# Taking 1 - beta of stick-breaking attention from the scores by a sigmoid of their negative

## The chip, the cores and the metric

The program is one decoder layer and runs on one core of a Trainium2 chip. The time is device microseconds (us) from the start of the program to its end. Below, TensorE is PE in the rows (its weight loads are PEld), ScalarE is ACT, VectorE is DVE, GpSimd is POOL and SyncE is SP.

## The reference, cut to what matters

A layer has three mixers (chunked gMLP, gated DeltaNet, stick-breaking attention), a gated merge and a feed-forward part. The change is in attention alone: 8 heads of 64, 1024 positions, swept in blocks of 128 queries.

```python
# A[t,s] = beta[t,s] prod_{s<j<t} (1-beta[t,j]), beta = sigmoid(q.k/sqrt(dh)), s<t
z = jnp.einsum('bthd,bshd->bhts', qi, kf) * scale          # scale = 64 ** -0.5
causal = kpos[None, :] < tpos[:, None]
log_keep = jnp.where(causal, jax.nn.log_sigmoid(-z), 0.0)
later = lax.cumsum(log_keep, axis=3, reverse=True) - log_keep
w = jnp.where(causal, jnp.exp(jax.nn.log_sigmoid(z) + later), 0.0)
return jnp.einsum('bhts,bshd->bthd', w, vf)
```

The kernel works with the products themselves. For each score it needs beta = sigmoid(z) and the factor that it calls keep, 1 - beta, which equals sigmoid(-z). A scan from the right multiplies the keeps, and beta times the product of the later keeps is the weight.

## The kernel before, in words

Weights come from HBM in 512 KB pieces, are split by ACT into an upper part (`w_hi`, L308) and by DVE into a rest (`w_lo`, L313), and each product of the large matrices is three matmuls (L321 to L323). These products run through the whole kernel. The other mixers' work is laid between them.

Attention is a loop of four passes, each over two heads (u = 0 and 1). A pass has 12 pieces of scores: the query blocks in `ORDER`, each with up to 512 keys, so 128 to 512 columns. All engines walk the same steps x = -2 to 12 of a pass, written out by hand, each in its own queue, and wait for each other through counting semaphores:

- PE (L1070 on): in step x the scores of piece x + 2 into `z0` and `z1` (`scores`, one PSUM bank for each head), in the first step also the transposes of v (`turn_values`) into `dn0` and `dn1`, the weighted values of piece x - 1 (`weighted_values`), a share of the matrix products (`pe_beside`), the transposes of piece x (`turn`), and another share of products. The banks `z0` and `z1` are single: from the second piece of a pass on `scores` waits at L1077 until the previous piece has been read. That is 11 waits in a pass, 44 in all.
- ACT (L769 on): `sigmoid` (L777) reads `z` and writes `a_b`, for both heads of piece x + 2. In the first step of a pass two copies of the turned values follow (L805, PSUM to `a_v`). Then `keep` (L784) reads `a_b` and writes `a_keep`, and for each head `take_turned` (L791) follows it and waits for the transposes of piece x. Then come the evictions of the products (L363) and the `w_hi` splits that fall due (`act_beside`).
- DVE (L1414 on): for piece x + 1 the two scans over `a_keep` (L1426), the two products with `a_b` (`weigh`, L1436), the mask, then the `w_lo` splits (`dve_beside`). At the end of a pass and between pieces it copies finished output (`take_y`, L1452).
- SP only loads weights and stores and loads projections. ACT sends the attention output away (L795).

`a_b`, `a_keep` and `a_A` have four buffers each, two pieces. At the start of each pass ACT has an `ACT_TABLE_LOAD` ahead of its first sigmoid.

Of the kernel before, what the change touches and what calls it, by code (L numbers as in the profile page):

```python
# [58 lines left out]
def hybrid_decoder_layer(nc, xT, w_stream, w_bd, w_spT, cols_in, consts_in, outT):  # L59
    f32, f32r, bf16 = mybir.dt.float32, mybir.dt.float32r, mybir.dt.bfloat16  # L60
    ACT, ALU = mybir.ActivationFunctionType, mybir.AluOpType
# [9 lines left out]
    def sb(name, shape, dt=f32):  # L71
        return scope[0].enter_context(nc.sbuf_tensor(name, shape, dt))

    def sem(name):
        return top.enter_context(nc.semaphore(name))

    with top:
# [71 lines left out]
        with scope[0]:  # L149
# [4 lines left out]
            a_b = [sb(f"a_b{s}", [P, HALF]) for s in range(4)]  # L154
            a_keep = [sb(f"a_keep{s}", [P, HALF]) for s in range(4)]
# [56 lines left out]
        def bank(name):  # L212
            return top.enter_context(nc.psum_tensor(name, [P, HALF], f32))

        g_bank = [bank("gemm0"), bank("gemm1")]
        z_bank = [bank("z0"), bank("z1")]
# [37 lines left out]
        z_ready, b_ready, keep_ready, p_ready, a_raw, a_ready = (  # L254
            sem(n) for n in ("z_ready", "b_ready", "keep_ready", "p_ready", "a_raw", "a_ready"))
# [218 lines left out]
        NST = 2 * NBK  # L474
        LEAD = 2
# [222 lines left out]
        def _(act):  # L698
# [70 lines left out]
            with act.Fori(0, 4) as i:  # L769
                b = Beside(PAIR_AT + 2 * i, AT_SLOTS, (ACT.Identity,) * 2)  # L770

                def sigmoid(y):
                    n = block_of(y // 2)[3]
                    act.wait_ge(z_ready, NST * i + y + 1)
                    if y >= 4:
                        act.wait_ge(a_ready, NST * i + y - 3)
                    nc.scalar.activation(a_b[y % 4][:, 0:n], z_bank[y % 2][:, 0:n], ACT.Sigmoid, scale=0.125).then_inc(b_ready, 1)  # L777

                def keep(y):
                    n = block_of(y // 2)[3]  # L780
                    act.wait_ge(b_ready, NST * i + y + 1)
                    if y >= 4:
                        act.wait_ge(p_ready, NST * i + y - 3)
                    nc.scalar.activation(a_keep[y % 4][:, 0:n], a_b[y % 4][:, 0:n], ACT.Identity, scale=-1.0, bias=1.0).then_inc(keep_ready, 1)  # L784

                def take_turned(y):
                    x, u = divmod(y, 2)
                    n = block_of(x)[3]
                    act.wait_ge(turned, NST * i + y + 1)
                    act.wait_ge(av_done, 1 + NBK * i + x - 1)  # L790
                    nc.scalar.activation(a_AT[u][x % 2][:, 0:n], d_bank[u][:, 0:n], ACT.Copy).then_inc(at_read, 1)  # L791

                def store_y(T):
                    act.wait_ge(av_read, 2 + 8 * i + (4 if T else 8))
                    act.dma_start(yT[8 + i, :, HALF * T:HALF * T + HALF], a_y[:, HALF * T:HALF * T + HALF]).then_inc(y_stored[T], 16)  # L795

                for x in range(-LEAD, NBK + 1):
                    if x + LEAD < NBK:
                        for u in range(2):
                            sigmoid(2 * (x + LEAD) + u)  # L800
                    if x == -LEAD:
                        for hf in range(2):
                            act.wait_ge(at_vt, 2 * i + hf + 1)
                            act.wait_ge(av_done, 1 + NBK * i)
                            nc.scalar.activation(a_v[:, 4 * hf:4 * hf + 4, :], d_bank[hf][:].rearrange("p (n c) -> p n c", c=P),  # L805
                                                 ACT.Copy).then_inc(at_v, 1)
                    for u in range(2):
                        if x + LEAD < NBK:
                            keep(2 * (x + LEAD) + u)
                        if 0 <= x < NBK:  # L810
                            take_turned(2 * x + u)
                    act_beside(act, b)
                    act_beside(act, b)
                    if x == LAST_OF[3] + 3:
                        store_y(1)
                store_y(0)
# [69 lines left out]
            for b in range(4):  # L886
                for hf in range(2):
                    x = 2 * b + hf
# [24 lines left out]
            for i in range(2):  # L913
                for q in range(6):
                    n, s = PAIR_BR + 3 * i + q // 2, q % 2
# [97 lines left out]
        def _(pe):  # L1013
# [56 lines left out]
            with pe.Fori(0, 4) as i:  # L1070
                b = Beside(PAIR_AT + 2 * i, AT_SLOTS, (ACT.Identity,) * 2)

                def scores(x):

                    blk, p, s0, n, off = block_of(x)
                    if x:
                        pe.wait_ge(b_ready, NST * i + 2 * x)  # L1077
                    for u in range(2):
                        h = slice(64 * u, 64 * u + 64)
                        nc.tensor.matmul(z_bank[u][:, 0:n], a_q[h, P * blk:P * blk + P], a_k[h, s0:s0 + n],  # L1080
                                         start=True, stop=True).then_inc(z_ready, 1)

                def turn_values():

                    pe.wait_ge(vT_loaded, 16 * i + 16)
                    pe.wait_ge(at_read, 1 + NST * i)
                    for hf in range(2):
                        for n in range(4):
                            last = nc.tensor.transpose(d_bank[hf][:, P * n:P * n + P], a_vT[:, P * (4 * hf + n):P * (4 * hf + n) + P], ident)
                        last.then_inc(at_vt, 1)  # L1090

                def turn(y):

                    x, u = divmod(y, 2)
                    n = block_of(x)[3]
                    pe.wait_ge(a_ready, NST * i + y + 1)
                    if x == 0:
                        pe.wait_ge(at_v, 2 * i + u + 1)
                    else:
                        pe.wait_ge(at_read, 1 + NST * i + y - 1)  # L1100
                    for m in range(n // P):
                        last = nc.tensor.transpose(d_bank[u][:, P * m:P * m + P], a_A[y % 4][:, P * m:P * m + P], ident)  # L1102
                    last.then_inc(turned, 1)

                def weighted_values(x):

                    blk, p, s0, n, off = block_of(x)
                    pe.wait_ge(at_read, 1 + NST * i + 2 * x + 2)
                    if newest(x):
                        pe.wait_ge(av_read, 2 + 8 * i + p - 1)  # L1110
                    for m in range(n // P):
                        for u in range(2):
                            last = nc.tensor.matmul(y_bank[p % 2][64 * u:64 * u + 64, 0:P], a_v[:, s0 // P + m, 64 * u:64 * u + 64],
                                                    a_AT[u][x % 2][:, P * m:P * m + P], start=(newest(x) and m == 0),
                                                    stop=(oldest(x) and m == n // P - 1), skip_group_check=True)
                    last.then_inc(av_done, 1)

                pe.wait_ge(at_loaded, 32 * i + 32)
                for x in range(-LEAD, NBK + 1):
                    if x + LEAD < NBK:  # L1120
                        scores(x + LEAD)
                    if x == -LEAD:
                        turn_values()
                    if x >= 1:
                        weighted_values(x - 1)
                    pe_beside(pe, b)
                    if 0 <= x < NBK:
                        turn(2 * x)
                        turn(2 * x + 1)
                    pe_beside(pe, b)  # L1130
            leave_phase(pe)

            with pe.Fori(0, 4) as i:
# [18 lines left out]
                for x, name in enumerate(DN_STAGES):  # L1152
                    for g in range(2):
# [10 lines left out]
                        for m in range(4):  # L1164
                            n = 4 * g + m
# [63 lines left out]
            for b in range(4):  # L1229
                pe.wait_ge(g_chain, 13 + 4 * b + 2)  # L1230
                for hf in range(2):
                    if b:
                        pe.wait_ge(g_act, 8 + 2 * b)
                    for m in range(4):
                        n = 4 * hf + m
# [15 lines left out]
            for i in range(2):  # L1251
                for q in range(6):
                    n, s = PAIR_BR + 3 * i + q // 2, q % 2
                    pe.wait_ge(lo_ready[s], n + 1)
                    for r in range(4):
# [3 lines left out]
                        for k in range(4):  # L1259
                            kk, y = 4 * dd + k, 4 * (q % 3) + k  # L1260
# [56 lines left out]
        def _(dve):  # L1317
# [96 lines left out]
            with dve.Fori(0, 4) as i:  # L1414
# [14 lines left out]
                def weigh(y):  # L1429

                    x, u = divmod(y, 2)
                    blk, p, s0, n, off = block_of(x)
                    dve.wait_ge(p_ready, NST * i + y + 1)
                    if y >= 4:
                        dve.wait_ge(turned, NST * i + y - 3)
                    nc.vector.tensor_tensor(a_A[y % 4][:, 0:n], a_b[y % 4][:, 0:n], a_P[u][p % 2][:, off + 1:off + n + 1],  # L1436
                                            ALU.mult).then_inc(a_raw if newest(x) else a_ready, 1)
# [145 lines left out]
            for b in range(4):  # L1583
# [5 lines left out]
                y = g_y[b % 2]  # L1589
                if b >= 2:  # L1590
                    dve.wait_ge(g_store[b % 2], 16)
                for hf in range(2):
                    t = slice(HALF * hf, HALF * hf + HALF)
                    dve.wait_ge(g_pe, 10 + 4 * b + 2 + hf + 1)
                    bias = cols[:, None, V_BSP + P * b:V_BSP + P * b + P].broadcast_to([P, 4, P])
# [8 lines left out]
            for i in range(2):  # L1604
                for q in range(6):
                    n, s = PAIR_BR + 3 * i + q // 2, q % 2
# [264 lines left out]
```

## Time and profile before

| | |
|---|---|
| Time, median of 3 runs (lowest, highest) | 2145.39 us (2144.16, 2149.23) |
| The profiled execution's own time | 2151.76 us |
| Its span | 2149.9 us |
| PE busy, share of the span | 2014.6 us, 94% |
| ACT busy | 765.0 us, 36% |
| DVE busy | 934.9 us, 43% |
| Mean granted TensorE clock | 0.975 |
| Attention, first to last scores | 167.1 to 464.8 us after the span's start |

Busy shares are averages over the whole layer. PE is close to full nearly everywhere, so an instruction elsewhere matters only if PE ends up waiting for it. The views of waits say for whom an engine waited, the timeline gives the order with starts and durations, and the views by stretch give the granted clock, where 1.00 is 2.4 GHz and 0.50 is 1.2 GHz.

### The profile page before, as it was taken

Reading aid. Unit: us, or ns where it says so; the run is one execution under the profiler, and the core shown is the slowest. Engines: PE = TensorE matmul, PEld = TensorE weight load, DVE = VectorE, ACT = ScalarE, POOL = GpSimd, SP = SyncE. Lnnn points to the kernel's source line nnn. Section 1 sums busy time; section 2 is a strip of 40 time slices with the busy share of each in tenths; the row PEclk is TensorE's granted clock in tenths of the full one; section 3 lists DMA queues with packets and bytes.
Section 4 is the critical chain, followed back from the end, with each engine's and each line's share of the span. In section 5 each row is a group of like instructions: output and inputs, shape, how many; then the busy total and the mean of one; then the engine's idle time right before and its main releaser. Section 6 shows DMA issues by size and latency. Waiting matters only on the chain.

```text
span 2149.9 us, 27155 instructions
## 1 busy us (share of the span) xinstructions
PE 2014.6 (94%) x9986; PEld 1610.2 (75%) x9986; DVE 934.9 (43%) x1291; ACT 765.0 (36%) x1176; POOL 77.1 (4%) x63
## 2 busy tenths in 40 slices
PE   7999999999999999998798997988999999999996
PEld 5886776677878778787486886766888888888875
DVE  5715456455344272442144553565323323322346
ACT  5325555444343343532134333444113202202331
POOL 0000000000202002030000000000000000000000
PEclk9999999999999999999899998989999999999998
DMA  4232222213021030211425444322211111111143
GB/s 167 98 108 70 86 76 73 88 59 137 21 94 72 29 117 21 96 39 49 176 99 196 138 137 147 118 95 92 69 49 47 52 49 39 52 46 49 49 166 118
DMA packets 59624, 186.95 MB, mean 87 GB/s; under 512 B 6448, under 2 KB 6448, under 8 KB 59568
## 3 DMA queue, kind: packets, MB, share of 16 engines
q1 hardware_dynamic: 56112, 179.91, 23.7%
q10 hardware_dynamic: 3456, 6.29, 0.8%
q8 instruction: 36, 0.59, 0.1%
q14 instruction: 20, 0.16, 0.0%
HBM read 140.04 MB, written 46.14 MB: 87 GB/s over the span
## 4 chain that ended last, share of the span: by engine, by line
PE 76%; DVE 8%; ACT 6%; DMA 5%; issue 5%; SPq 1%; DVEq 0%; ACTq 0%
PE gemm L321 16%; PE gemm L323 15%; PE gemm L322 15%; DMA w_raw<-w_stream 3%; PE gemm L536 3%; PE gemm L537 3%; PE gemm L538 3%; PE dn L1184 2%; ACT w_hi L308 2%; PE z L1080 2%; PE dn L1182 2%; PE gemm L1263 2%; PE gemm L1264 2%; PE gemm L1265 2%; PE dn L1102 1%
## 5 line engine op out<-in xcount | busy, mean ns | idle before, releaser
L321 PE MATMUL gemm<-act_hi,w_hi 128*128 128x512 f32 x1216 | 513.6, 422 | 7.8 <-ACT stage L363 7.1
L323 PE MATMUL gemm<-act_hi,w_lo 128*128 128x512 f32 x1216 | 478.8, 394 | 0.0
L322 PE MATMUL gemm<-act_lo,w_hi 128*128 128x512 f32 x1216 | 477.8, 393 | 0.0
L313 DVE TENSOR_TENSOR w_lo<-w_raw,w_hi 128x1024 fp32r<-128x1024 f32 x166 | 204.5, 1232 | 403.8 <-ACT w_hi L308 399.9
L308 ACT ACTIVATE w_hi<-w_raw 128x1024 fp32r<-128x1024 f32 x166 | 174.8, 1053 | 342.3 <-PE gemm L323 229.9
L321 PEld LDWEIGHTS gemm<-act_hi,w_hi 128*128 128x128 f32 x1216 | 231.4, 190 | 67.9 <-issue 21.3
L323 PEld LDWEIGHTS gemm<-act_hi,w_lo 128*128 128x128 f32 x1216 | 230.1, 189 | 50.2
L322 PEld LDWEIGHTS gemm<-act_lo,w_hi 128*128 128x128 f32 x1216 | 231.5, 190 | 44.3 <-issue 6.5
L363 ACT ACTIVATE stage<-gemm,cols 128x512 f32<-128x512 f32 x104 | 71.2, 685 | 230.8 <-PE gemm L323 224.9
L321 PE MATMUL gemm<-f_hi,w_hi 128*128 128x512 f32 x384 | 149.5, 389 | 0.0
L323 PE MATMUL gemm<-f_hi,w_lo 128*128 128x512 f32 x384 | 149.5, 389 | 0.0
L322 PE MATMUL gemm<-f_lo,w_hi 128*128 128x512 f32 x384 | 149.5, 389 | 0.0
L536 PE MATMUL gemm<-act_hi,w_hi 128*128 128x512 f32 x256 | 107.6, 420 | 32.6 <-DVE w_lo L313 21.7
L965 ACT ACTIVATE f_t<-f_t 128x512 f32<-128x512 f32 x64 | 40.3, 630 | 203.3 <-DVE f_t L1686 203.3
L1426 DVE TENSOR_TENSOR_SCAN a_P<-a_keep,a_P,a_floor 128x512 f32<-128x512 f32 (+3 forms) x96 | 93.9, 1006 | 29.5 <-ACT a_keep L784 29.4
L537 PE MATMUL gemm<-act_lo,w_hi 128*128 128x512 f32 x256 | 103.5, 404 | 0.0
L538 PE MATMUL gemm<-act_hi,w_lo 128*128 128x512 f32 x256 | 103.1, 403 | 0.0
L1789 POOL TENSOR_TENSOR d_bB<-d_at,consts 128x512 f32<-128x512 f32 x48 | 64.3, 1354 | 888.8 <-DVE d_at L1535 801.6
L1686 DVE SCALAR_TENSOR_TENSOR f_t<-gemm,sum_x 128x512 f32<-128x512 f32 x64 | 44.2, 691 | 110.1 <-PE gemm L323 91.3
L1692 DVE TENSOR_TENSOR f_lo<-f_t,f_hi 128x512 f32 (+1 forms) x64 | 44.3, 693 | 102.2 <-ACT f_hi L967 102.2
L536 PEld LDWEIGHTS gemm<-act_hi,w_hi 128*128 128x128 f32 x256 | 50.4, 197 | 50.3 <-DVE w_lo L313 25.1
L1263 PE MATMUL gemm<-y_hi,w_hi 128*128 128x512 f32 x192 | 77.4, 403 | 9.0 <-DVE y_lo L404 7.7
(247 smaller groups left out, 2950.5 us busy)
## 6 DMA issues: line engine op xcount, KB each, us to landing
w_raw<-w_stream SPq DMA_DIRECT2D x166, 512.0 KB, 3.5
projections<-stage SPq DMA_DIRECT2D x60, 512.0 KB, 2.9
gate<-projections SPq DMA_DIRECT2D x48, 256.0 KB, 2.7
d_in<-projections SPq DMA_DIRECT2D x12, 512.0 KB, 5.0
y_lo<-branch_outputs SPq DMA_DIRECT2D x6, 1024.0 KB, 12.0
x_sb<-xT SPq DMA_DIRECT2D x8, 512.0 KB, 9.6
x_fin<-xT SPq DMA_DIRECT2D x8, 512.0 KB, 8.5
residual<-mixed ACTq DMA_DIRECT2D x16, 256.0 KB, 2.0
```

What stands on the lines that cost most here:

```text
L308: nc.scalar.activation(hi[s][:], raw[s][:].rearrange("p (k c) -> p k c", k=KT), ACT.Copy).then_inc(hi_ready[s], 1)
L313: nc.vector.tensor_tensor(lo[s][:], raw[s][:].rearrange("p (k c) -> p k c", k=KT), hi[s][:].bitcast(f32), ALU.subtract).then_inc(lo_ready[ ...
L321: nc.tensor.matmul(g_bank[hf][:], w_hi[s][:, k, :], a_hi[:, k, t], start=(k == 0), stop=False)
L322: nc.tensor.matmul(g_bank[hf][:], w_hi[s][:, k, :], a_lo[:, k, t], start=False, stop=False)
L323: last = nc.tensor.matmul(g_bank[hf][:], w_lo[s][:, k, :], a_hi[:, k, t], start=False, stop=(k == KT - 1))
L363: nc.scalar.activation(stage[s][:, HALF * hf:HALF * hf + HALF], g_bank[hf][:], func, bias=cols[:, ds(V_BIN + 2 * n + s, 1)]).then_inc(bank ...
L536: nc.tensor.matmul(g_bank[s][:], w_hi[s][:, k, :], a_hi[:, k, t], start=(k == 0), stop=False)
L537: nc.tensor.matmul(g_bank[s][:], w_hi[s][:, k, :], a_lo[:, k, t], start=False, stop=False)
L538: last = nc.tensor.matmul(g_bank[s][:], w_lo[s][:, k, :], a_hi[:, k, t], start=False, stop=(k == KT - 1))
L1263: nc.tensor.matmul(g_bank[hf][:], w_hi[s][:, kk, :], y_upper(y)[:, t], start=(k == 0), stop=False)
L1426: nc.vector.tensor_tensor_scan(run[:, off:off + n][:, ::-1], a_keep[y % 4][:, 0:n][:, ::-1], floor[:, ::-1], run[:, off + n:off + n + 1], ...
L1789: nc.gpsimd.tensor_tensor(d_B[:, c, :], d_at[:, c, :], consts[:, None, C_LEV + lev, :].broadcast_to([P, 4, P]), ALU.mult).then_inc(dn_b[g], 1)
```

## The change

`keep` is now a sigmoid of the scores times -0.125, read from PSUM like beta, and no longer an affine function of `a_b`. It waits for `z_ready` and not for `b_ready`. On ACT the calls of `sigmoid` and `keep` change places, so that both keeps of a piece come first and the betas follow. PE must wait for both before it overwrites `z`, and DVE's `weigh` waits for `b_ready` itself.

```diff
@@ ACT, in the loop of the four passes @@
                 def keep(y):
                     n = block_of(y // 2)[3]
-                    act.wait_ge(b_ready, NST * i + y + 1)
+                    act.wait_ge(z_ready, NST * i + y + 1)
                     if y >= 4:
                         act.wait_ge(p_ready, NST * i + y - 3)
-                    nc.scalar.activation(a_keep[y % 4][:, 0:n], a_b[y % 4][:, 0:n], ACT.Identity, scale=-1.0, bias=1.0).then_inc(keep_ready, 1)
+                    nc.scalar.activation(a_keep[y % 4][:, 0:n], z_bank[y % 2][:, 0:n], ACT.Sigmoid, scale=-0.125).then_inc(keep_ready, 1)
...
                 for x in range(-LEAD, NBK + 1):
                     if x + LEAD < NBK:
                         for u in range(2):
-                            sigmoid(2 * (x + LEAD) + u)
+                            keep(2 * (x + LEAD) + u)
                     if x == -LEAD:
...
                     for u in range(2):
                         if x + LEAD < NBK:
-                            keep(2 * (x + LEAD) + u)
+                            sigmoid(2 * (x + LEAD) + u)
                         if 0 <= x < NBK:
                             take_turned(2 * x + u)
@@ PE, scores @@
                     if x:
                         pe.wait_ge(b_ready, NST * i + 2 * x)
+                        pe.wait_ge(keep_ready, NST * i + 2 * x)
@@ DVE, weigh @@
                     dve.wait_ge(p_ready, NST * i + y + 1)
+                    dve.wait_ge(b_ready, NST * i + y + 1)
```

ACT at the start of the first pass, before. `a_b` is beta, `a_v` the turned values, `dn` the banks with the transposes:

```order
L777 ACT_TABLE_LOAD
L777 ACTIVATE a_b0<-z0 128x128 [waits z_ready]
L774 REGISTER_ALU
L777 ACTIVATE a_b1<-z1 128x128 [waits z_ready]
L803 ISA
L804 ISA [waits at_vt]
L805 ACTIVATE a_v<-dn0 128x512 [waits av_done]
L803 REGISTER_ALU
L805 ACTIVATE a_v<-dn1 128x512 [waits av_done,at_vt]
L784 ACTIVATE a_keep0<-a_b0 128x128 [waits b_ready]
L784 ACTIVATE a_keep1<-a_b1 128x128 [waits b_ready]
```

The same place of ACT in the changed kernel:

```order
L784 ACT_TABLE_LOAD
L784 ACTIVATE a_keep0<-z0 128x128 [waits z_ready]
L781 REGISTER_ALU
L784 ACTIVATE a_keep1<-z1 128x128 [waits z_ready]
L803 ISA
L804 ISA [waits at_vt]
L805 ACTIVATE a_v<-dn0 128x512 [waits av_done]
L803 REGISTER_ALU
L805 ACTIVATE a_v<-dn1 128x512 [waits av_done,at_vt]
L777 ACTIVATE a_b0<-z0 128x128 [waits z_ready]
L777 ACTIVATE a_b1<-z1 128x128 [waits z_ready]
```

The last reader of `z0` and `z1` stood ahead of the two copies to `a_v` and now stands behind them.

ACT in the third step of a pass (x = 0), before. `a_AT` is the transposed weights of piece 0:

```order
L774 REGISTER_ALU
L777 ACTIVATE a_b0<-z0 128x256 [waits a_ready,z_ready]
L774 REGISTER_ALU
L777 ACTIVATE a_b1<-z1 128x256 [waits a_ready,z_ready]
L784 ACTIVATE a_keep0<-a_b0 128x256 [waits p_ready,b_ready]
L791 ACTIVATE a_AT00<-dn0 128x128 [waits av_done,turned]
L784 ACTIVATE a_keep1<-a_b1 128x256 [waits p_ready,b_ready]
L791 ACTIVATE a_AT10<-dn1 128x128 [waits av_done,turned]
```

The same step of ACT in the changed kernel:

```order
L781 REGISTER_ALU
L784 ACTIVATE a_keep0<-z0 128x256 [waits p_ready,z_ready]
L781 REGISTER_ALU
L784 ACTIVATE a_keep1<-z1 128x256 [waits p_ready,z_ready]
L777 ACTIVATE a_b0<-z0 128x256 [waits a_ready,z_ready]
L791 ACTIVATE a_AT00<-dn0 128x128 [waits av_done,turned]
L777 ACTIVATE a_b1<-z1 128x256 [waits a_ready,z_ready]
L791 ACTIVATE a_AT10<-dn1 128x128 [waits av_done,turned]
```

The second beta, a reader of `z1`, now stands where the second keep stood, behind the copy that waits for PE's transposes.

PE at the second scores of a pass, before:

```order
L323 MATMUL gemm0<-act_hi,w_lo0 128x512
L1077 REGISTER_ALU
L1080 MATMUL z0<-a_k,a_q 128x512 [waits b_ready]
L1080 MATMUL z1<-a_k,a_q 128x512
L321 MATMUL gemm0<-act_hi,w_hi0 128x512
```

And PE there in the changed kernel, one line further down in the file:

```order
L323 MATMUL gemm0<-act_hi,w_lo0 128x512
L1077 REGISTER_ALU
L1081 MATMUL z0<-a_k,a_q 128x512 [waits keep_ready,b_ready]
L1081 MATMUL z1<-a_k,a_q 128x512
L321 MATMUL gemm0<-act_hi,w_hi0 128x512
```

PE's order stays; the first matmul of the scores waits for two semaphores.

## Rows read from the trace of the kernel before

**Rows 1.** The page, busy us, share of the span, instructions.
```profile
PE 2014.6 (94%) x9986; PEld 1610.2 (75%) x9986; DVE 934.9 (43%) x1291; ACT 765.0 (36%) x1176; POOL 77.1 (4%) x63
```

**Rows 2.** By stretch, first and last pass: length, engines' busy us, PEclk, DMA, GB/s.
```profile
165.00:242.00 77.00, 76.25 (x467) 54.63 (x466) 44.59 (x82) 41.35 (x87) 0.00 (x0) 1.00 0.22 80
...
396.00:473.00 77.00, 75.25 (x456) 54.05 (x454) 43.39 (x75) 40.90 (x85) 0.00 (x0) 0.98 0.16 58
```

**Rows 3.** Waits of PE, 160 to 480 us: total us, times, longest.
```profile
PE z L1080 <- ACT a_b L777: 5.7, 4, 1.8
```

**Rows 4.** Waits of ACT, 160 to 480 us.
```profile
ACT a_AT L791 <- PE dn L1102: 84.0, 48, 2.5
...
ACT L777 <- DVE a_y L1452: 7.2, 3, 2.4
```

**Rows 5.** Waits of DVE, 160 to 480 us.
```profile
DVE w_lo L313 <- ACT w_hi L308: 103.4, 17, 9.3
DVE a_P L1426 <- ACT a_keep L784: 29.4, 24, 3.9
```

**Rows 6.** Timeline of ACT, start of pass 1: start us, us, what.
```profile
171.30 0.45 ACT L777 ACTIVATE a_b<-z 128x128 f32<-128x128 f32 x2
...
172.59 0.53 ACT L784 ACTIVATE a_keep<-a_b 128x128 f32<-128x128 f32 x2
```

**Rows 7.** Timeline of ACT, start of pass 2; in brackets idle before, releaser.
```profile
247.57 1.28 ACT L777 ACT_TABLE_LOAD   x1 [2.41 <-DVE a_y L1452]
248.86 0.45 ACT L777 ACTIVATE a_b<-z 128x128 f32<-128x128 f32 x2
249.19 1.09 ACT L805 ACTIVATE a_v<-dn 128x512 f32<-128x512 f32 x2
250.15 0.53 ACT L784 ACTIVATE a_keep<-a_b 128x128 f32<-128x128 f32 x2
```

**Rows 8.** Timeline of PE, second scores of each of the four passes.
```profile
171.80 1.13 PE L1080 MATMUL z<-a_k,a_q 64*128 64x512 f32 x4 [0.41 <-ACT a_b L777]
...
249.36 1.13 PE L1080 MATMUL z<-a_k,a_q 64*128 64x512 f32 x4 [1.77 <-ACT a_b L777]
...
326.90 1.13 PE L1080 MATMUL z<-a_k,a_q 64*128 64x512 f32 x4 [1.75 <-ACT a_b L777]
...
404.48 0.70 PE L1080 MATMUL z<-a_k,a_q 64*128 64x512 f32 x2 [1.75 <-ACT a_b L777]
```

**Rows 9.** The tiles `a_b` and `a_keep`, durations ns: least, median, most.
```profile
L777 ACT ACTIVATE a_b<-z x96: 272/551/628, 171.3 to 465.3; 128x512 f32<-128x512 f32 x48, 128x128 f32<-128x128 f32 x16, 128x256 f32<-128x256 f32 x16, 128x384 f32<-128x384 f32 x16
L784 ACT ACTIVATE a_keep<-a_b x96: 302/588/669, 172.6 to 468.5; 128x512 f32<-128x512 f32 x48, 128x128 f32<-128x128 f32 x16, 128x256 f32<-128x256 f32 x16, 128x384 f32<-128x384 f32 x16
```

**Rows 10.** Timeline of ACT, third step of pass 2.
```profile
257.83 0.28 ACT L791 ACTIVATE a_AT<-dn 128x128 f32<-128x128 f32 x1 [0.73 <-PE dn L1102]
258.01 0.41 ACT L784 ACTIVATE a_keep<-a_b 128x256 f32<-128x256 f32 x1
```

**Rows 11.** Timeline of PE's weight loads, fourth scores of pass 2.
```profile
258.54 0.30 PEld L1080 LDWEIGHTS z<-a_k,a_q 64*128 64x128 f32 x4 [0.36 <-issue]
```

**Rows 12.** By stretch, columns as in rows 2: five stretches behind an idle PE.
```profile
249.37:255.41 6.04, 6.04 (x26) 4.16 (x27) 4.86 (x10) 4.01 (x9) 0.00 (x0) 1.00 0.00 1
326.91:332.99 6.08, 6.08 (x26) 4.16 (x27) 4.90 (x10) 4.00 (x9) 0.00 (x0) 1.00 0.00 1
404.49:412.14 7.65, 7.65 (x26) 5.33 (x26) 5.30 (x10) 4.00 (x9) 0.00 (x0) 0.78 0.00 1
...
499.39:506.20 6.81, 6.81 (x19) 5.39 (x20) 6.36 (x6) 3.57 (x4) 0.00 (x0) 0.59 0.19 77
...
1180.09:1186.90 6.81, 6.74 (x22) 5.12 (x23) 4.17 (x5) 1.21 (x2) 0.00 (x0) 0.75 0.14 43
```

**Rows 13.** Timeline of PE, the matmuls that open two of those stretches.
```profile
499.38 0.79 PE L321 MATMUL gemm<-act_hi,w_hi 128*128 128x512 f32 x1 [4.62 <-ACT stage L363]
...
1180.08 0.51 PE L1263 MATMUL gemm<-y_hi,w_hi 128*128 128x512 f32 x1 [1.50 <-DVE y_lo L404]
```

## The prediction

> **What bounds the kernel now.** I read the page first: TensorE is busy 94% of the span and ScalarE 36% [rows 1], so a ScalarE instruction counts only where TensorE waits for it. The view by stretch, laid over the passes of attention, says the same of the place of the change: of the first pass's 77.00 us TensorE is busy 76.25, ScalarE 41.35, VectorE 44.59, and the last pass differs only in its clock [rows 2]. The views of waits came next. In attention TensorE waits for other engines in one place alone, the scores: 5.7 us in 4 waits, all for beta [rows 3]. ScalarE spends 84.0 us waiting for TensorE's transposes [rows 4], VectorE 103.4 us for `w_hi` and 29.4 us for `a_keep` [rows 5]; none of that is passed on. The timeline then shows that the 4 waits are the second scores of each pass, with 0.41, 1.77, 1.75 and 1.75 us of idle TensorE ahead of them [rows 8]. There ScalarE goes through a table load, two betas, two copies to `a_v`, two keeps [rows 6, 7], and TensorE starts when the second beta is done: the pair ends at 248.86 + 0.45 = 249.31, the scores begin at 249.36, so 0.05 us pass from release to start.
>
> **The operation itself.** Per piece two affine functions from SBUF become two sigmoids from PSUM, 96 instructions in all. For equal shapes the nearest row is beta, which is the same instruction already: 272 against 302 ns for the shortest, 551 against 588 for the median [rows 9]. That is 0.03 to 0.04 us less each, 3 to 4 us of ScalarE's time, and nothing for the end, since ScalarE waits 84.0 us for transposes anyway. If that cover were gone, the 3 to 4 us would be a gain and no loss. The table load stays one in a pass: both versions call the sigmoid first.
>
> **The order on ScalarE at the start of a pass.** This is the term that costs. The last reader of `z0` and `z1` was the second beta, ahead of the copies; it becomes the second beta behind them. The second keep stands there now: in pass 1 the pair ends at 172.59 + 0.53 = 173.12, in pass 2 at 250.15 + 0.53 = 250.68 [rows 6, 7]. Taking off 0.03 for the shorter instruction and adding 0.05 for the release, the scores begin at 173.14 and 250.70 instead of 171.80 and 249.36 [rows 8]: 1.34 us later. From the other side, with the measured length of a beta pair instead: 250.15 + 0.45 + 0.05 = 250.65, 1.29 us later. TensorE is idle already at that point, so all of it adds, and in pass 1 too. Four passes give 5.2 to 5.4 us; I take 5.3. The copies themselves wait for nothing new. What stands behind the waiting scores in TensorE's queue is matrix products, and everybody else in the pass waits on TensorE, so nothing makes the time good later. ScalarE's release at the start of the next pass hangs on the last `a_y` copy [rows 4], which follows TensorE as well.
>
> **The order on ScalarE inside a pass.** The keeps come first where the betas stood, and the betas take the keeps' places. The second beta now stands behind the copy to `a_AT` that waits for TensorE's transposes. The other 40 scores wait for it. The narrowest place that I found is the fourth scores of a pass: the copy begins at 257.83, the second keep at 258.01 and ends at 258.42 [rows 10], and the weights of the scores load at 258.54 [rows 11]. That leaves 0.12 us, less 0.05 for the release, plus 0.03 for the shorter instruction: 0.10 us to spare. So 40 waits at nothing. Covered they are by the products between the transposes and the next scores; without that cover each would cost what its beta is late, and the upper bound that I keep is one release, 0.05 us, at each of 40, so 2.0 us.
>
> **The added waits.** TensorE's wait for `keep_ready` is satisfied before the one for `b_ready`, since both keeps are done ahead of the first beta; nothing. VectorE's `weigh` waits for beta, which comes two scans later than it needs; its scans can start about one beta pair earlier, up to 1.1 us, and VectorE's 29.4 us of waiting for `a_keep` shrinks. TensorE never waits for `a_A` in attention [rows 3], so I put this at nothing too, and below nothing only by the rival at the end.
>
> **The clock.** The granted clock is no constant. Behind the 1.75 us of idle in pass 4 it was 0.78 in the mean over 7.65 us, where the same 26 matmuls of pass 2, behind 1.77 us of idle, took 6.04 us at 1.00 [rows 8, 12]. So a fall to 1.2 GHz costs 7.65 - 6.04 = 1.6 us, and it came once in three such gaps. Behind 1.50 us elsewhere it was 0.75 over 6.81 us, which is (1 - 0.75) x 6.81 = 1.7 us, and behind 4.62 us it was 0.59, or 2.8 us [rows 12, 13]. The change lengthens the gaps of passes 2 to 4 to 3.1 us and that of pass 1 to 1.7 us. I expect a fall behind each of the three, 3 x 1.6 = 4.8, a third of one in pass 1, 0.5, and take off the 1.6 that this execution has already paid: +3.7 us. The ends are no fall at all, -1.6, and four falls at 2.8, 11.2 - 1.6 = +9.6.
>
> The Trainium skill speaks of this in "TensorE: Matmul & The Clock Gate", section "HAM oscillation": its rule of thumb names a length of idle gap beyond which the engine starts again at the low clock, and the gaps forecast here stay below it. By that rule there would be no clock term, and the sum would be about 5 us. The trace bears it out in two passes of three and not in pass 4, where a shorter gap was followed by a fall. It is among the rivals. Another page speaks against the change altogether: "Perfetto Trace Analysis", section "Optimizing Tensor Performance", wants independent matmul groups to rotate through PSUM banks so that the eviction of one overlaps the next. Holding `z` for a second read goes against that at each of the 44 scores, and by the rule I would have counted a beta pair, 1.1 us, at each, some 48 us; the rows say that ScalarE's second read is in time at 40 of them.
>
> **The sum.** 5.3 + 3.7 = 9.0 us on the profiled execution's 2151.76 us (span 2149.9 and 1.86 around it), so 2160.8. The median of the runs lies 6.4 us lower, and the change should add about the same there: 2145.39 + 9.0 = 2154.4. A measurement of this kernel can tell a change from none beyond about 0.3%, here 6.4 us.
>
> **The rivals.**
> - The clock does not answer to the longer gaps: only the 5.3 us of waiting are added, 2150.7. For it: two of three gaps of 1.75 us went without a fall [rows 12]. Against: behind 1.50 us it fell elsewhere, and 3.1 is twice that. Chance 0.22; this case is within 0.3%.
> - The added wait is hidden, because the release of the second scores does not come from the place in the queue that I read, or is given back where TensorE waits later: 0 us, 2145.4. Against: TensorE is already idle at this point in all four passes [rows 8]. Chance 0.07.
> - Betas late inside the pass too: the 0.10 us margin fails and TensorE waits at the 40 inner scores. At 0.05 each 2 us, and if ScalarE runs a tenth of a microsecond or more late, 4 to 6: 9.0 + 5 = 14, 2159.4. For it: the narrow margin. Against: the place of the second keep was in time each time. Chance 0.08.
> - Faster: VectorE, with its scans earlier, finishes a pass earlier, and the last `a_y` copy, for which ScalarE's start of the next pass waits 7.2 us in all [rows 4], comes forward so far that the second scores wait no more. Then the four gaps of 5.7 us and the one fall of 1.6 go: -7.3, 2138.1. It turns into a gain only once the copy comes more than 1.3 us earlier. Against: at the end of a pass VectorE waits for `w_hi` and the copy stands behind that, which the scans don't touch. Chance 0.03.
> - The forecast itself, +9.0 within 7 to 12: chance 0.60.
>
> Slower by over 0.3%: 0.60 + 0.08 and a little of the first rival's upper part, less a little of the forecast's lower part, 0.67. Within 0.3%: 0.30. Faster: 0.03. The range goes from 2148.0, which keeps most of the case without clock term, to 2160.5, which takes in falls of 2.8 us; the outer bounds worked out above are +3.6 and +17.0 (5.4 + 9.6 + 2.0).
>
> **What would show it.** At the second scores of each pass the gap ahead of TensorE is 1.7 us in pass 1 and 3.1 us in passes 2 to 4, and its releaser is beta; the total of that wait is near 11 us instead of 5.7. The granted clock of the stretch behind is near 0.78 in passes 2 to 4, and the stretch about 7.6 us long. Keeps have beta's durations. ScalarE's row order at a pass start is keeps, `a_v`, betas. VectorE's wait for `a_keep` shrinks, and its work ends no sooner in the passes. No other scores wait. I am wrong if the first gap stays, if any of the other 40 scores waits for `a_b`, or if TensorE waits anywhere else that it did not.

## The result, and the profile after

| | before | changed |
|---|---|---|
| Time, median (lowest, highest) | 2147.31 us (2144.16, 2150.97), 4 runs | 2167.14 us (2166.14, 2170.39), 4 runs |
| Ratio, 95% interval | | 1.0094 (1.0073 to 1.0116) |
| Profiled execution: time, span | 2151.76, 2149.9 us | 2167.50, 2165.7 us |
| Attention, first to last scores | 297.50 us | 311.65 us |
| The rest of the span | 1852.4 us | 1854.1 us |

The change made the kernel 19.8 us slower, where 9.0 were forecast; the range ended at 2160.5. The direction was right and the size was not. A second measurement, below, gave 1.0064 (1.0050 to 1.0077), or 14.3 us. Attention is counted from the start of the first scores in pass 1 to the start of the last scores in pass 4.

The first line is the page's, for [rows 1]:

```profile
PE 2020.4 (93%) x9986; PEld 1612.3 (74%) x9986; DVE 934.6 (43%) x1291; ACT 762.9 (35%) x1176; POOL 77.2 (4%) x63
```

ScalarE's busy time fell by 2.1 us, as cheaper keeps should make it. TensorE's rose by 5.8 us with the same number of instructions: the same matmuls took longer. In attention alone its busy time went from 291.81 to 300.66 us, 8.9 more. That is the first sign of the clock.

The waits of PE, ACT and DVE in the changed kernel between 160 and 495 us (total us, times, longest), for [rows 3 to 5]:

```profile
PE z L1081 <- ACT a_b L777: 11.0, 4, 3.1
```
```profile
ACT a_AT L791 <- PE dn L1103: 85.4, 48, 2.6
...
ACT L784 <- DVE a_y L1454: 7.2, 3, 2.4
```
```profile
DVE a_P L1427 <- ACT a_keep L784: 29.6, 12, 3.8
...
DVE a_A L1438 <- ACT a_b L777: 3.2, 8, 0.5
```

TensorE still waits for beta in 4 places, now for 11.0 us in place of 5.7: 5.3 more, the forecast's first term to the tenth. Timelines of PE at the second scores and of ACT ahead of those of pass 2, for [rows 7, 8]:

```profile
174.28 0.70 PE L1081 MATMUL z<-a_k,a_q 64*128 64x512 f32 x2 [1.75 <-ACT a_b L777]
...
254.77 1.22 PE L1081 MATMUL z<-a_k,a_q 64*128 64x512 f32 x2 [3.09 <-ACT a_b L777]
...
336.55 1.22 PE L1081 MATMUL z<-a_k,a_q 64*128 64x512 f32 x2 [3.07 <-ACT a_b L777]
...
418.38 1.22 PE L1081 MATMUL z<-a_k,a_q 64*128 64x512 f32 x2 [3.07 <-ACT a_b L777]
```
```profile
251.66 1.28 ACT L784 ACT_TABLE_LOAD   x1 [2.41 <-DVE a_y L1454]
252.95 0.45 ACT L784 ACTIVATE a_keep<-z 128x128 f32<-128x128 f32 x2
253.28 1.09 ACT L805 ACTIVATE a_v<-dn 128x512 f32<-128x512 f32 x2
254.24 0.48 ACT L777 ACTIVATE a_b<-z 128x128 f32<-128x128 f32 x2
```

Keeps, copies, betas: the betas end at 254.24 + 0.48 = 254.72 and the scores start at 254.77. What was not forecast is in the view by stretch. Each row goes from the second scores to the third, for [rows 12] (length, busy us by engine, then PEclk, DMA, GB/s):

```profile
174.28:181.94 7.66, 7.66 (x26) 5.31 (x26) 4.43 (x8) 2.75 (x5) 0.00 (x0) 0.78 0.03 11
254.77:263.74 8.97, 8.97 (x26) 5.84 (x26) 4.42 (x8) 2.76 (x5) 0.00 (x0) 0.65 0.00 0
336.55:345.57 9.02, 9.02 (x26) 5.85 (x26) 4.42 (x8) 2.75 (x5) 0.00 (x0) 0.64 0.00 0
418.38:427.44 9.06, 9.06 (x26) 5.88 (x26) 4.42 (x8) 2.75 (x5) 0.00 (x0) 0.64 0.00 0
```

The work of a stretch takes 6.04 us at full clock. Here the four take 34.71 us, 10.6 more than 4 x 6.04 = 24.16. Before, the four stretches took 25.82 us, 1.6 more, for one fall. So 34.71 - 25.82 = 8.9 us come from the clock, and 5.3 + 8.9 = 14.2 is the difference of attention, 311.65 - 297.50. The rest of the two spans differs by 1.7 us.

### The profile page after: what moved, and what is told of

Its sections match the earlier page's. It is cut to its first block, busy times and chain, and to the rows that moved or that the text cites. A ratio compares the mean times of both kernels' runs of the same rounds, so it can differ in the third digit from the quotient of the medians.

```text
span 2165.7 us, 27215 instructions
## 1 busy us (share of the span) xinstructions
PE 2020.4 (93%) x9986; PEld 1612.3 (74%) x9986; DVE 934.6 (43%) x1291; ACT 762.9 (35%) x1176; POOL 77.2 (4%) x63
## 4 chain that ended last, share of the span: by engine, by line
PE 75%; DVE 8%; ACT 6%; issue 5%; DMA 5%; SPq 1%; DVEq 0%; ACTq 0%
PE gemm L321 16%; PE gemm L323 15%; PE gemm L322 15%; DMA w_raw<-w_stream 3%; PE gemm L536 3%; PE gemm L538 3%; PE gemm L537 3%; PE dn L1185 2%; PE z L1081 2%; ACT w_hi L308 2%; PE dn L1183 2%; PE gemm L1264 2%; PE gemm L1265 2%; PE gemm L1266 2%; DVE d_cv L1491 1%
## 5 line engine op out<-in xcount | busy, mean ns | idle before, releaser
L1427 DVE TENSOR_TENSOR_SCAN a_P<-a_keep,a_P,a_floor 128x512 f32<-128x512 f32 (+3 forms) x96 | 92.2, 1002 | 29.6 <-ACT a_keep L784 29.6
```

Source lines behind the costliest of these rows:

```text
L1427: nc.vector.tensor_tensor_scan(run[:, off:off + n][:, ::-1], a_keep[y % 4][:, 0:n][:, ::-1], floor[:, ::-1], run[:, off + n:off + n + 1], ...
```

## The experiments

Theory A: the last reader of `z` stands behind the two copies at the start of a pass, TensorE idles longer there, and the granted clock falls behind the longer gap. Rivals: B, a price inside the pass (the second read of PSUM, the second wait, betas behind the transposes' copies); C, the exchange of places as such; D, another cause of the long stretches; E, one fixed cost. Times "within 3 us of the changed kernel" are told by ratios to the kernel before in the same measurement. The changed kernel has two of them, 1.0094 and 1.0064. The second ran on one chip with the moved products, the first four experiments on another, and of the first the chip is not on record.

### Betas ahead of the copies

```diff
                     if x == -LEAD:
+                        for u in range(2):
+                            sigmoid(u)
                         for hf in range(2):
                             act.wait_ge(at_vt, 2 * i + hf + 1)
...
-                        if x + LEAD < NBK:
+                        if x > -LEAD and x + LEAD < NBK:
                             sigmoid(2 * (x + LEAD) + u)
```

> The changed kernel, with one difference: in the first step of a pass the two betas come ahead of the two copies to a_v (keeps, betas, copies). Everything inside the pass is as in the changed kernel. Theory A (the loss is the place of the last reader of z at the start of a pass, and the clock that answers to the longer gap): the second scores are released by the second beta, two short instructions or 0.35 us later than in the kernel before, so TensorE's wait for beta at the four second scores is 5.7 + 4 x 0.35 = 7.1 us instead of 11.0, the stretch behind each is 6.0 to 7.7 us instead of 9.0, and the time is +2 to +7 us on the kernel before, 12 to 17 below the changed kernel. Theory B (the loss comes from inside the pass: two reads of PSUM, the second wait of the scores, betas behind the transposes' copies): nothing of that is altered, so the time stays within 3 us of the changed kernel.

Measured: 2148.72 us against 2147.12, ratio 1.0005 (0.9994 to 1.0016). Waits of PE, and the stretch from second to third scores in passes 2 and 3:

```profile
PE z L1083 <- ACT a_b L777: 7.1, 4, 2.1
```
```profile
246.11:252.15 6.04, 6.04 (x26) 4.16 (x26) 4.76 (x9) 3.68 (x7) 0.00 (x0) 1.00 0.00 0
323.98:330.02 6.04, 6.04 (x25) 4.17 (x25) 4.77 (x9) 3.69 (x7) 0.00 (x0) 1.00 0.00 0
```

The wait is the 7.1 us that theory A gave, and the clock did not fall behind any of the four gaps. The time came out a little better than its +2. That there was no fall was luck, since the kernel before has one in each of its traces behind shorter gaps. Attention took 297.19 us: the 297.50 of before, 1.4 of added waiting, and 1.6 less for the fall that did not come, within 0.1. Everything inside the pass was as in the changed kernel, so this takes B's place away: all that the change does there costs nothing that can be measured.

### Keep from the scores, in its old place

```diff
 def keep(y):
-    act.wait_ge(b_ready, NST * i + y + 1)
+    act.wait_ge(z_ready, NST * i + y + 1)
-    nc.scalar.activation(a_keep[y % 4][:, 0:n], a_b[y % 4][:, 0:n], ACT.Identity, scale=-1.0, bias=1.0)
+    nc.scalar.activation(a_keep[y % 4][:, 0:n], z_bank[y % 2][:, 0:n], ACT.Sigmoid, scale=-0.125)
 # PE, scores: waits for b_ready and keep_ready; DVE, weigh: waits for b_ready; order on ACT as before
```

> The kernel before with keep as a sigmoid of the negated scores from PSUM, but in its old place behind beta (and behind the copies to a_v at the start of a pass). TensorE waits for both, as in the changed kernel. Theory A: the last reader of z stands behind the copies here too, so it costs the same as the change: wait at the second scores 11 us, stretches behind of 9.0 us in passes 2 to 4, time within 3 us of the changed kernel. If the exchange of places on ScalarE by itself were what costs (theory C), this kernel would stay within 3 us of the kernel before.

Measured: 2160.23 us, ratio 1.0059 (1.0040 to 1.0079). Waits of PE, and the four stretches:

```profile
PE z L1081 <- ACT a_keep L784: 11.0, 4, 3.1
```
```profile
170.51:176.55 6.04, 6.04 (x25) 4.16 (x25) 4.73 (x10) 2.76 (x5) 0.00 (x0) 1.00 0.06 24
249.39:257.05 7.66, 7.66 (x25) 5.33 (x25) 5.10 (x10) 2.75 (x5) 0.00 (x0) 0.78 0.00 0
329.87:338.81 8.94, 8.94 (x26) 5.80 (x26) 5.10 (x10) 2.75 (x5) 0.00 (x0) 0.65 0.00 0
411.62:420.64 9.02, 9.02 (x26) 5.85 (x26) 5.10 (x10) 2.75 (x5) 0.00 (x0) 0.65 0.00 0
```

Same wait, same kind of stretches, without the exchange of places. The stretch of pass 2 is 7.66 us where 9.0 was written down, and pass 1 has no fall. The time is within 3 us of the changed kernel by its second measurement, 1.0064, and not by its first, 1.0094. C is out even so, since it wanted the time of the kernel before: it does not matter which of the two stands last, only that the last one stands behind the copies.

### The wait alone

```diff
 # kernel before, PE, scores
     pe.wait_ge(b_ready, NST * i + 2 * x)
+    pe.wait_ge(keep_ready, NST * i + 2 * x)
```

> The kernel before, with one wait added: the scores on TensorE also wait for the previous piece's keep, which here is still the affine function of beta in SBUF, so no value depends on the wait. No second read of PSUM, no exchange of places. Theory A: the wait is released by the second keep behind the copies, 1.37 us after beta, so TensorE waits 11.1 us at the second scores and the time is within 3 us of the changed kernel (+18 to +22 us). Theory B (reading PSUM twice, or the sigmoid in place of the affine function): this kernel keeps the time of the kernel before, within 3 us.

Measured: 2162.78 us (2158.18 to 2166.74), ratio 1.0062 (1.0042 to 1.0082): 15.7 us slower, less than the 18 to 22 written down, which leaned on the first measurement of the change. Waits of PE, and the stretches of passes 1 and 2:

```profile
PE z L1081 <- ACT a_keep L784: 11.5, 4, 3.2
```
```profile
174.00:181.62 7.62, 7.62 (x25) 5.30 (x25) 4.98 (x10) 2.81 (x5) 0.00 (x0) 0.78 0.04 13
254.64:263.36 8.72, 8.72 (x26) 5.61 (x26) 4.98 (x10) 2.81 (x5) 0.00 (x0) 0.67 0.00 0
```

One wait, with no second read of PSUM and no new sigmoid, costs as much as the whole change: its attention takes 311.65 us, as the changed kernel's did. That the two agree to the hundredth is chance, for this kernel waits 0.5 us longer and its four stretches sum to 33.98 us instead of 34.71. B is out in its other half too.

### The changed kernel with the gap filled

```diff
 # PE, end of a step
     pe_beside(pe, b)
+    if x == -LEAD:
+        pe.wait_ge(av_read, 2 + 8 * i - 1)
+        for _ in range(10):
+            nc.tensor.matmul(o_bank[:], act_hi[:, 0, 0:P], act_hi[:, 0, 0:HALF], start=True, stop=True)
```

> The changed kernel, with 10 matmuls 128x128 by 512 added on TensorE between the first step's products and the second scores of each pass; their result goes to the idle output bank and is overwritten. They add 10 x 0.227 = 2.3 us of work and take no value. If the larger part of the loss is the clock that falls behind the gap (theory A), the gap falls from 3.1 to 0.8 us in passes 2 to 4 and vanishes in pass 1, where the scores start 0.5 us later; the stretch behind, from the second to the third scores, goes from 9.0 us to 6.0 in passes 2 to 4 and from 7.7 to 6.0 in pass 1; the time is 8 to 11 us below the changed kernel although TensorE does more. If the long stretches have another cause (ScalarE or a bank late behind the second scores, theory D), they stay at 9.0 and the time is the same as the changed kernel or up to 2 us longer.

Measured: 2152.80 us, ratio 1.0024 (1.0013 to 1.0035), against the changed kernel's 1.0064 in its second measurement: 0.4% or 8.6 us less, with 40 matmuls more. On its own chip it is 7.4 and 10.0 us below the two kernels that have the same wait, 1.0059 and 1.0062. Waits of PE, and two stretches:

```profile
PE z L1081 <- ACT a_b L777: 2.4, 3, 0.8
```
```profile
173.40:179.46 6.06, 6.06 (x26) 4.16 (x26) 3.98 (x6) 2.76 (x5) 0.00 (x0) 1.00 0.01 3
252.29:258.33 6.04, 6.04 (x25) 4.17 (x25) 4.42 (x8) 2.76 (x5) 0.00 (x0) 1.00 0.00 0
```

ScalarE's queue is the changed kernel's, the scores start as late as there, and the long stretches are gone: the clock was behind them, not a late bank (D). Attention takes 301.58 us, the sum of 295.9 (before without its fall), the 5.3 of the wait and the 0.4 us by which the filling overshoots in pass 1. That is 4.1 us over the attention of before, which has a fall to pay. The medians differ by 5.7 us, with an interval from 2.8 to 7.5 that takes in the 4.1.

### The changed kernel and the kernel before again

> The changed kernel once more, unaltered, for its spread on the chip that also runs the next kernels, and for a second trace. Waiting is fixed by the program and the clock is not: the gaps at the second scores are 1.75, 3.1, 3.1, 3.1 us again, the stretch behind each is 6.0, 7.7 or 9.0 us, and the executions spread over several us. Against the kernel before +11 to +21 us. If instead the change has one fixed cost (theory E), the executions lie within 3 us of each other at +18 to +20.

Measured: 2162.19 us (2160.88 to 2164.44, 6 runs) against 2147.84 (24 runs), ratio 1.0064 (1.0050 to 1.0077). Its four stretches:

```profile
171.06:177.11 6.05, 6.05 (x26) 4.17 (x26) 4.42 (x8) 2.76 (x5) 0.00 (x0) 1.00 0.06 22
249.94:257.61 7.67, 7.67 (x26) 5.30 (x26) 4.42 (x8) 2.75 (x5) 0.00 (x0) 0.78 0.00 0
330.42:339.44 9.02, 9.02 (x25) 5.85 (x26) 4.42 (x8) 2.75 (x5) 0.00 (x0) 0.64 0.00 0
412.26:421.32 9.06, 9.06 (x25) 5.88 (x26) 4.42 (x8) 2.75 (x5) 0.00 (x0) 0.64 0.00 0
```

Same program, same 11.0 us of waiting, attention 308.75 us: 2.9 us less than in the first trace, all of it clock in passes 1 and 2. Its executions lie within 3.6 us of each other, close to the 3 that E wrote down, but at +13 to +17 and not at +18 to +20; the two traces differ by 2.9 us of clock under the same program, so the cost is not one number.

> The kernel before, unaltered, for a second trace. The gaps at the second scores are fixed by the program: 0.41, 1.77, 1.75, 1.75 us. The clock behind them is not: none, one or two stretches of 7.7 us instead of 6.0, so attention from first to last scores takes 295.9 us plus 1.6 for each fall (the first trace: 297.5 with one).

> The kernel before a third time, for the same: 295.9 us plus 1.6 for each fall. If both new traces show no fall, the profiled execution that the prediction rested on was dearer in attention than most.

Measured, one execution each: 2149.48 and 2151.41 us. The stretch that fell, pass 3 in the first and pass 4 in the second:

```profile
327.28:334.91 7.63, 7.63 (x26) 5.34 (x26) 5.29 (x10) 4.02 (x9) 0.00 (x0) 0.78 0.00 0
```
```profile
403.66:411.30 7.64, 7.64 (x25) 5.30 (x25) 5.29 (x10) 4.01 (x9) 0.00 (x0) 0.78 0.00 0
```

Attention took 297.43 and 297.48 us, with one fall each. All three traces of the kernel before agree, so the execution that the prediction rested on was an ordinary one in attention.

### Products moved ahead of the second scores

```diff
-        AT_SLOTS = [2.0, 2.0, 3.0, 3.0]
+        AT_SLOTS = [3.0, 4.0, 2.0, 1.0]   # kernel before; and first experiment's kernel
+        AT_SLOTS = [4.0, 4.0, 1.0, 1.0]   # changed kernel
```

`AT_SLOTS` holds the weights by which the product steps of a pass are shared out. A step of the loop has two shares, so the first two weights stand ahead of the second scores and the next two between the second and the third.

> The kernel before with the first four shares of products in a pass weighted 3, 4, 2, 1 instead of 2, 2, 3, 3. Three of the 64 product steps (0.68 us each, 2.04 us) move from behind the second scores of a pass to ahead of them; nothing else moves. Theory A: beta is ready before TensorE arrives, so the four gaps (0.41 and three of 1.75) close, 5.7 us go, and with them the falls of the clock behind them, one of 1.6 us in the profiled execution of before; the third scores still have 1.7 us to spare. -5.7 to -8 us on the kernel before, and every stretch at full clock. Rival: the products only move, and TensorE waits for beta at the third scores instead: 0 us.

> The first experiment's kernel (keeps, betas, copies at the start of a pass, the change as it is everywhere else) with the same three steps of products moved ahead of the second scores. The gaps there were 0.75 and 2.1 us, the cover is 2.04 us, so 0.1 us is left in three passes. The third scores wait for the last beta, which has 2.7 - 2.04 = 0.7 us to spare. So -5 to -8 us on the kernel before, within 1 us of the kernel before with the same move. If the sigmoid from PSUM or the second wait has a price of its own that the clock has covered so far, it shows here as a difference of over 2 us between the two.

> The changed kernel with five steps of products (3.4 us) moved ahead of the second scores (weights 4, 4, 1, 1). The gap of 3.1 us there closes. But only 2 steps are left between the second and the third scores, and the last beta had 2.7 us to spare there with 7: 2.7 - 3.4 leaves TensorE waiting 0.7 us for beta at the third scores of each pass, a new wait of 2.8 us in all in place of 11.0. Gaps that short bring no fall of the clock. So -5.7 + 2.8 = -3 us on the kernel before (between -1 and -5), some 15 below the changed kernel.

| kernel | median us | ratio to before (95%) | attention us | gaps at second, third scores, pass 2 |
|---|---|---|---|---|
| before, moved | 2142.53 | 0.9966 (0.9952 to 0.9979) | 289.91 | 0, 0 |
| betas first, moved | 2144.11 | 0.9981 (0.9968 to 0.9995) | 290.30 | 0.07, 0 |
| changed, moved | 2143.49 | 0.9977 (0.9965 to 0.9989) | 292.40 | 0, 0.56 |

PE in the changed kernel with products moved, the second and third scores of pass 2, and its waits:

```profile
251.07 1.13 PE L1081 MATMUL z<-a_k,a_q 64*128 64x512 f32 x4
254.34 0.70 PE L1081 MATMUL z<-a_k,a_q 64*128 64x256 f32 x4 [0.56 <-ACT a_b L777]
```
```profile
PE z L1081 <- ACT a_b L777: 2.3, 4, 0.6
```

The 3.1 us gap is gone and a wait of 0.56 us appears at the next scores in each pass, 2.3 in all where 2.8 were written down. In the kernel before the gaps close without a new one and attention shrinks by 7.6 us, 5.7 of waiting and 1.6 of clock and 0.3 besides. Its median fell by 5.3 only, under the 5.7 to 8 expected; the interval goes from 4.5 to 10.3 us and takes in the 7.6, so the shortfall is not clear of noise. It has the lowest median found, 0.34% below the kernel before, though the intervals of the three overlap. The second kernel has the change's keep with no fall of the clock in attention that could cover a price: 0.4 us more in attention than the first, of which three gaps of 0.07 are seen. Its median, 3.7 us below the kernel before, missed its -5, and it stands 1.6 above the first where 1 was written down; that is under the 2 us that would have spoken for a price of the keep, and the two intervals overlap.

The third kernel, the changed one, is 4.4 us below the kernel before, in its range of 1 to 5, and 18.7 below the changed kernel on the same chip, where 15 were written down. In attention it is 2.5 us over the first, and its new waits of 2.3 us are nearly all of that.

## Why the prediction was wrong

- **The operation itself.** Right in its sign and in its effect on the end. The median keep fell from 588 to 556 ns. ScalarE's busy time fell by 2.1 us and not by 3 to 4; the median beta became longer, 562 ns for 551, which was not forecast.
- **The order at the start of a pass.** Right: 5.3 us forecast, 11.0 - 5.7 = 5.3 measured, at the four second scores and nowhere else. Shown by the first three experiments: the copies between the last two readers of `z` make it, whichever reader is last.
- **The order inside a pass.** Right: TensorE waits at none of the other 40 scores. In pass 2's third step of the changed kernel the second beta, on ACT, and the fourth scores, on PE's weight loads, stand so:

```profile
266.34 0.38 ACT L777 ACTIVATE a_b<-z 128x256 f32<-128x256 f32 x1
```
```profile
266.87 0.30 PEld L1081 LDWEIGHTS z<-a_k,a_q 64*128 64x128 f32 x4 [0.36 <-ACT a_b L777]
```

  That is 0.15 us from end to start, or 0.10 to spare, as worked out. The row names beta as the releaser, because it came last, but the 0.36 us ahead of the weight load were there before with "issue" [rows 11]: a releaser in a row is not yet a wait. The view of waits counts 8 such entries for the weight loads and only 4 for the matmuls.
- **The added waits.** Nothing at the end, right; one detail wrong. VectorE's waiting for `a_keep` did not shrink: 29.4 became 29.6 us, since what its earlier scans gained inside the passes came back at their starts, where VectorE waits for a later TensorE.
- **The clock. This is the step that failed.** I wrote "I expect a fall behind each of the three, 3 x 1.6 = 4.8". The falls came, all three, and a fourth in pass 1. But I had taken the price of a fall from the one behind a gap of 1.75 us. Behind 3.1 us the clock was low for longer: the stretches of 8.97, 9.02 and 9.06 us have lost 2.9 to 3.0 us each. The trace shows how. In pass 1 the granted clock is 1.00 when the scores start at 174.28 and 0.50 from 175.7 to 179.1. In pass 2 it is 0.51 from 254.20 to 254.70, while TensorE is still idle, and back at 1.00 only at 261.0; the first two matmuls of the scores take 1.22 us there, against 0.70 in pass 1. The two gaps of 3.1 us that cost only 1.6, in pass 2 of the second trace and of the second experiment, went as pass 1 did. The term was +3.7 and measured +8.9 in the first trace and +6.0 in the second. The row of 4.62 us of idle with its 2.8 us of loss was in my list [rows 12, 13], as the bound, and there too the clock was low before TensorE started, at 0.50 from 498.50 to 499.00. The 3.1 us lie nearly as near to 4.62 as to 1.75, and the value should have stood between, 3 x 2.2, which would still have been short of the first trace's. The rule of thumb of the Trainium skill ("TensorE: Matmul & The Clock Gate", section "HAM oscillation"), which I had as a rival, would have had no fall at all. The traces speak against it: behind gaps of 3.07 to 3.23 us the clock fell 12 times in 12, in four traces of three kernels.
- **What the sum leaves open.** With the measured clock term the sum is 5.3 + 8.9 = 14.2 us for the first trace and 5.3 + 6.0 = 11.3 for the second, against 19.8 and 14.3 between the medians. The first measurement's two traces differ by 15.7 in time. The profiled execution of before lay 4.5 us above its median and the changed one's 0.4. That closes the sum of the first measurement, but not the cause; the 3.0 us that are left of the second are not traced either. In the twelve traces of this study the span outside attention, whose code no kernel altered, lies between 1845.2 and 1855.2 us, and the changed kernel's two at 1854.1 and 1850.6. The low clock stands at other places there from one execution to the next: in the three traces of the kernel before, its mean from 1400 to 1450 us is 0.83, 0.83 and 0.90. Whether the change shifts the odds of that, for instance because all that follows comes later, isn't settled, and the intervals of the two measured ratios, 1.0094 and 1.0064, only just overlap.

## What to carry to other kernels

Where a bank has one copy, the last reader's place in its engine's queue is its release; before a second reader is added, look at what stands between the two readers, at the start of each loop above all, where the steady state says nothing. An idle gap of TensorE can have a second price in the clock behind it, and here it did not grow in proportion: 1.3 us more of gap brought up to 3.0 us of clock in a pass. So price a lengthened gap by the row of a gap of that length, and look there whether the clock is already low when the work starts again. And a gap that one queue can't close may be closed by moving work of TensorE's own ahead of it, as long as enough stays behind for the next wait.

## What the runs showed of the hardware

Whether the granted clock fell behind a short gap changed from one execution of a program to the next; behind the longer ones it fell each time. Of 16 gaps of 1.74 to 2.11 us at the second scores 5 were followed by a fall, each of 1.6 us; of the 12 gaps of 3.07 to 3.23 us all were, 2 at 1.6 and 10 at 2.7 to 3.0 us; of the gaps of 0.83 us and less none. In the falls that cost 1.6 us the clock was full when TensorE started again and fell 0.9 to 1.5 us later; in the ten others it was low 0.3 to 1.2 us before TensorE started and stayed so twice as long. Filling the 3.1 us gaps with 10 matmuls each whose result nobody reads made the kernel faster by more than half of what the change had added, 8.6 of 13.7 us by the ratios.
